# Group norm of a retention branch moved to GpSimd for both token tiles, with new orders in the third block

## The reference

```python
def chunkwise_retention(q, k, v):           # 8 heads of 64
    ...
    scores = jnp.einsum('bihd,bjhd->bhij', qc, kc) * inner_decay[None]
    ...

y = chunkwise_retention(qr, kr, vr)
mu = jnp.mean(y, axis=-1, keepdims=True)
var = jnp.mean(jnp.square(y - mu), axis=-1, keepdims=True)
y = ((y - mu) * lax.rsqrt(var + GN_EPS)).reshape(b, s, B_WIDTH)
y = y * ret_gn_w[l].astype(jnp.float32) + ret_gn_b[l].astype(jnp.float32)
out_b = (jax.nn.silu(gb.astype(jnp.float32)) * y).astype(x.dtype)
x = x + jnp.concatenate([out_a, out_b], axis=-1) @ w_out[l]
```

## Time and profile before

| what | before |
|---|---|
| device time, median of 3 runs (lowest, highest) | 911.14 us (911.08, 912.14) |
| the profiled execution | 912.54 us, of which the span from first to last instruction is 910.8 us |
| mean granted TensorE clock | 0.998 of full speed |
| PE busy | 900.0 us (99% of the span) |
| DVE busy | 608.3 us (67%) |
| ACT busy | 489.0 us (54%) |
| POOL busy | 65.5 us (7%) |
| HBM traffic | 177 GB/s over the span |

### The profile page before, as it was taken

One profiled execution on the slowest core, in us unless ns is written; L12 is line 12 of the kernel. 1 busy time (PEld: TensorE's weight loads), 2 busy tenths in 40 slices (PEclk: granted clock), 3 DMA queues, 4 the chain that ended last, 5 costly groups with the idle time before them and its releaser, 6 DMA issues.

```text
span 910.8 us, 13492 instructions
## 1 busy us (share of the span) xinstructions
PE 900.0 (99%) x4811; PEld 755.2 (83%) x4811; DVE 608.3 (67%) x927; ACT 489.0 (54%) x755; POOL 65.5 (7%) x124
## 2 busy tenths in 40 slices
PE   9999999999999999999999999999998999999998
PEld 8778788888888887768888888888886888888887
DVE  5868867555555687874755555668998666555565
ACT  7666756444444475873644444555577554444442
POOL 1311112000000010000200000012320000000000
PEclk9999999999999999999999999999999999999999
DMA  8935155655555551436755555436361446555541
GB/s 294 344 133 182 56 189 204 207 185 184 185 190 192 172 185 46 167 134 233 254 199 193 184 184 188 154 128 230 95 208 47 139 142 229 184 185 194 189 169 47
DMA packets 96884, 159.88 MB, mean 176 GB/s; under 512 B 5968, under 2 KB 37920, under 8 KB 96840
## 3 DMA queue, kind: packets, MB, share of 16 engines
q1 hardware_dynamic: 94240, 155.08, 51.1%
q10 hardware_dynamic: 2568, 4.21, 1.4%
q0 software_dynamic: 32, 0.02, 0.0%
HBM read 158.21 MB, written 3.16 MB: 177 GB/s over the span
## 4 chain that ended last, share of the span: by engine, by line
PE 94%; DVE 4%; ACT 1%; issue 1%; POOL 0%; DVEq 0%; POOLq 0%; ACTq 0%
PE turn L1754 10%; PE proj L1754 9%; PE proj L1698 6%; PE score L1698 6%; PE proj L1700 6%; PE proj L1699 6%; PE score L1699 6%; PE score L1700 6%; PE outp L1698 5%; PE outp L1700 5%; PE outp L1699 5%; PE turn L1758 5%; PE proj L1758 5%; PE turn L1744 2%; PE score L1896 1%; PE turn L1906 1%
## 5 line engine op out<-in xcount | busy, mean ns | idle before, releaser
L2027 DVE TENSOR_TENSOR wlo<-raw,whi 128x2048 fp32r<-128x2048 f32 (+1 forms) x131 | 297.2, 2278 | 167.5 <-ACT whi L1449 132.7
L1449 ACT ACTIVATE whi<-raw 128x2048 fp32r<-128x2048 f32 x64 | 122.7, 1917 | 162.6 <-PE turn L1758 76.2
L1438 ACT ACTIVATE whi<-raw 128x2048 fp32r<-128x2048 f32 (+1 forms) x67 | 126.2, 1895 | 60.7 <-PE score L1700 17.0
L1698 PE MATMUL proj<-whi,set 128*128 128x512 f32 (+2 forms) x266 | 104.9, 394 | 0.0
L1700 PE MATMUL proj<-whi,set 128*128 128x512 f32 (+2 forms) x266 | 102.2, 384 | 0.0
L1699 PE MATMUL proj<-wlo,set 128*128 128x512 f32 (+2 forms) x266 | 102.0, 383 | 0.0
L1754 PE MATMUL turn<-set,whi 128*128 128x512 f32 x384 | 96.3, 393 | 0.0
L1754 PE MATMUL proj<-set,whi 128*128 128x512 f32 x384 | 95.6, 391 | 0.0
L1698 PE MATMUL score<-whi,set 128*128 128x512 f32 x232 | 91.5, 394 | 0.0
L1699 PE MATMUL score<-wlo,set 128*128 128x512 f32 x232 | 90.6, 391 | 0.0
L1700 PE MATMUL score<-whi,set 128*128 128x512 f32 x232 | 90.4, 390 | 0.0
(11 more groups left out here) (252 smaller groups left out, 1283.9 us busy)
## 6 DMA issues: line engine op xcount, KB each, us to landing
raw<-in_a_w_up SPq DMA_DIRECT2D x32, 512.0 KB, 4.2
raw<-in_a_w_down SPq DMA_DIRECT2D x32, 512.0 KB, 4.5
raw<-in_b_w_up SPq DMA_DIRECT2D x32, 512.0 KB, 4.2
raw<-in_b_w_down SPq DMA_DIRECT2D x32, 512.0 KB, 4.6
raw<-in_w_gate SPq DMA_DIRECT2D x22, 512.0 KB, 4.0
raw<-in_w_up SPq DMA_DIRECT2D x22, 512.0 KB, 5.0
raw<-in_w_down SPq DMA_DIRECT2D x22, 512.0 KB, 3.9
raw<-in_a_w_in SPq DMA_DIRECT2D x20, 512.0 KB, 6.5
```

The lines of the kernel that those rows point to most:

```text
L1438: return act.activation(shaped(whi, u)[:, ks, :], shaped(raw, u)[:, ks, :], ACT.Copy)
L1449: act.activation(shaped(whi, u), shaped(raw, u), ACT.Copy).then_inc(hi_done, 1)
L1698: pe.matmul(out_, hi, wh, start=start, stop=False)
L2027: return dve.tensor_tensor(shaped(wlo, u)[:, ks, :], shaped(raw, u)[:, ks, :], shaped(whi, u)[:, ks, :], ALU.subtract)
```

## The change

The inverse root of the group norm (both tiles, 16 columns) goes from DVE to POOL, into the same function that the other statistics use, so a wait of POOL on DVE's sums and a wait of DVE on POOL's result are added. Weight, bias and gate of tile 1 go from DVE to POOL too, behind those of tile 0. And the orders of PE, DVE and ACT in the third block are different.

```diff
@@ in the list of steps @@
         group = add("group_square")
+        inverse_use(group)
         group.o, group.va, group.rs = last[1], col(16), col(16)
@@ POOL @@
                 elif st.kind == "shared_key_sum":
                     inverse_of_sums(st.st, st.st.rs, st.st.ss, DH)
+                elif st.kind == "group_sum":
+                    inverse_of_sums(st.st, st.st.rs, st.st.va, DH, GN_EPS)
                 elif st.kind == "group_gate":
-                    y = o_nat[:, 0, 512:1024]
-                    pool.wait_ge(yn_done, 1)
                     pool.wait_ge(gn_landed, 32)
-                    behind(pool.tensor_tensor(y, y, gn[:, 0, :], ALU.mult))
-                    behind(pool.tensor_tensor(y, y, gn[:, 1, :], ALU.add))
-                    pool.wait_ge(*st.st.gate)
-                    pool.tensor_tensor(y, y, zq[:, 1, 0, :], ALU.mult).then_inc(ob_done, 1)
+                    for t in range(NT):
+                        y = o_nat[:, t, 512:1024]
+                        pool.wait_ge(yn_done, t + 1)
+                        behind(pool.tensor_tensor(y, y, gn[:, 0, :], ALU.mult))
+                        behind(pool.tensor_tensor(y, y, gn[:, 1, :], ALU.add))
+                        pool.wait_ge(*st.st.gate)
+                        pool.tensor_tensor(y, y, zq[:, 1, t, :], ALU.mult).then_inc(ob_done, 1)
@@ DVE @@
                         ins = dve.tensor_reduce(group.va[:, 8 * t:8 * t + 8], heads_view(rt[:, t, :]), AX_X, ALU.add)
-                    behind(ins)
-                    inverse_rms(group.rs, group.va, DH, GN_EPS)
+                    ins.then_inc(sum_done, 1)
                 elif st.kind == "group_scale":
                     group = st.st
+                    wait_inverse(group)
                     for t in range(NT):
                         y = heads_view(o_nat[:, t, 512:1024])
                         dve.tensor_tensor(y, y, spread(group.rs[:, 8 * t:8 * t + 8], DH), ALU.mult).then_inc(yn_done, 1)
-                elif st.kind == "group_gain":
-                    y = o_nat[:, 1, 512:1024]
-                    dve.wait_ge(yn_done, 2)
-                    dve.wait_ge(gn_landed, 32)
-                    behind(dve.tensor_tensor(y, y, gn[:, 0, :], ALU.mult))
-                    behind(dve.tensor_tensor(y, y, gn[:, 1, :], ALU.add))
-                elif st.kind == "group_gate":
-                    y = o_nat[:, 1, 512:1024]
-                    dve.wait_ge(*st.st.gate)
-                    dve.tensor_tensor(y, y, zq[:, 1, 1, :], ALU.mult).then_inc(ob_done, 1)
@@ MOVES, two entries of many @@
-        ("turn_weights 32", "turn_weights 33"), ("multiply 70", "multiply 71"), ("turn_heads 27", "multiply 69"),
+        ("turn_weights 32", "turn_weights 33"), ("keep_busy 1", "turn_weights 32"), ("multiply 70", "multiply 71"),
```

## The result

The changed kernel takes 913.68 us (median of 19 executions, 912.91 to 914.84) against 912.14 us for the kernel before (19, 911.08 to 913.88): a ratio over all executions of 1.0019, 95% interval [1.0013, 1.0025]. By the medians it is 1.5 us slower where 1.3 us faster was forecast. The profiled execution took 914.48 us around a span of 912.7, against 912.54 around 910.8.

What follows compares the result with a forecast made beforehand. PE, busy 99% of the span, was taken as the bound, so only its waits or low clock could be won. 0.95 us at `multiply 72` plus 0.4 at weight transposes gave 1.3 off 911.14: 909.8 us, range 908.2 to 912.1.

Steps and rivals of the forecast that it cites:

- The DVE part: Ahead of `scores 16`: without Newton and the products, three search rounds from 674.8 and the scale leave DVE free 5.0 us earlier.
- POOL's inverse: Group norm's inverse root: power of 0.69 to 5.5 us at 16 columns, taken as within the 1.6 us covered, no cost.
- The third rival: Slower: POOL's power grows with its columns to 5.5 us, delaying scale, y and `multiply 72`; 913.2 us, chance 0.11.
- The cover: At the transposes of y: ACT comes for y at 689.3, at least 0.8 us after PE has it.
- Scores 16 come later: At `scores 16`: ACT's query copies stand behind the gate's first tile, a new wait of 0.55 us.
- From there to the output projection: `scores 16` to `multiply 72`: PE waits 1.3 us, not 2.07, then ACT's queue sets the pace; `multiply 72` 0.95 us earlier.
- The surplus of 0.4: At the eight weight transposes at 703.05: 1.46 us falls to 1.04 without ACT's weight copy there, 0.4 us won.
- Group norm on POOL: POOL's six products start where they did, at 679.58, and take 8.2 us, ending at 687.7 to 688.5; no cost.
- The other moves: Reordered steps ahead of the query transposes, bias loads and `statistics 6`: taken as zero, up to 0.5 us each if cover fails.
- the clock's price: After PE's idle, from 686 to 690: the low clock withheld at most 1.0 + 0.56 us of work.
- The total: Whole kernel: 1.3 us off the median of 911.14 gives 909.8 us.
- the median's smaller surroundings: Whole kernel: time outside the span taken as smaller in the 911.14 median than in the profiled execution, 912.54 around 910.8.

Runs made afterwards that it cites:

- e3: Changed kernel with GpSimd's power over 2 of the 16 columns, the other 14 inverse roots set to 1: 912.28 us, ratio to before 1.0006.
- e8: Changed kernel with 12 more identity transposes on TensorE in its wait for GpSimd's y: 913.34 us, ratio to before 1.0012.
- e1: Changed kernel's code with the whole table of orders of the kernel before: 913.77 us, ratio to before 1.0017.
- e11: Changed kernel with the orders of before up to the last projections ahead of `scores 16`, new orders behind: 912.36 us, ratio to before 1.0009.
- e9: Kernel before with 25 instead of 10 keep-busy transposes on TensorE ahead of `scores 17`: 911.23 us, ratio 1.0002.
- e5: Changed kernel with the inverse back on VectorE and the old orders, all six products still on GpSimd: 912.15 us, ratio to before 0.9997.
- e10: e5 with 6 and 7 more transposes on TensorE in its two waits ahead of the mixed weights' transposes: 912.20 us, ratio to before 1.0005.
- e12: e11 with ScalarE's copy of query head 29 as before, so only the late orders are new: 913.23 us, ratio to before 1.0018.
- e6: Changed kernel with GpSimd's power over 2 of the 16 columns and the old orders: 912.40 us, ratio to before 1.0003.
- e13: Kernel before, unedited, profiled once more: this execution took 913.10 us.
- e7: Changed kernel with GpSimd's power of 16 columns done twice: 917.30 us, ratio to before 1.0051.
- e14: e12 unedited, profiled once more: this execution took 912.15 us.

## Why the prediction was wrong

**The DVE part** held in its lengths, not in its start: the rounds take 0.98 each, from 675.88 and not 674.8 (0.37 is the start of the program, the rest the early moves). They end at 678.8, and the maxima begin as soon as the scores are there. That VectorE was free early was worth 1.12 us at `scores 17`.

**POOL's inverse** is the step that failed: "I take a power within that, no cost". It took 2.91 us where the rounds cover 1.6, and PE waited 1.59 us for y. With the power over 2 columns 0.80 us of `multiply 76` is won (e3 against e8, both at full clock), and 0.79 us of time. Between 2 and 16 columns a power costs (2.91 - 0.69)/14 = 0.16 us a column on top of some 0.37. I had bounds of 0.69 and 5.5 and took a value by likeness to other instructions (VectorE's small ones, a GpSimd product of 512 columns), none of which is a power. The only row on a power had 2 columns and could not tell a fixed cost from one by column.

**The third rival** had the right mechanism (the power, the scale behind it, y late, then a low clock), with the size of the power too high and, more to the point, the length from which it decides: not some 4 us, since 2.9 was enough. The cover had been counted as if nothing else were late.

**Scores 16 come later** (0.36 of wait, 0.5 forecast) and **From there to the output projection** up to ScalarE's chain (wait 1.26, forecast 1.3; table load ended at 684.06, weight copy 1.90) held in shape. Then the chain was no longer ScalarE's: y came late, its operand copy waited 1.18 us, and `multiply 72` came 1.28 later in place of 0.95 earlier. The surplus of 0.4 at the eight weight transposes went where it was (1.46 at 703.05 before, 1.09 at 705.15 now), but the eight at 699.93 take 1.46 now; with the clock kept (e8) both take 1.09.

**Group norm on POOL** failed at its start. "It starts where it did" assumed the loads where they were; they are issued when PE has turned the queries, which the early moves delayed by 0.46, and with a cheap power GpSimd started on them 0.57 later (e3). The power added 0.85. The length of the six products was right: 8.45, forecast 8.1 to 8.9. The cover of 0.8 us was smaller than the 1.42 of the late start, and the late turn then brought the low clock.

**The other moves**, taken as nothing, are the second step that failed. They cost 0.46 us at the turn of the queries (e1 and e11 against the changed kernel): inside the 0 to 0.5 named for each, at its bad end. The forecast looked for the cost at PE alone; through the loads and the sums it grew to 0.90 us of time at full clock (e11), as much as the power's. One part is visible, PE's wait of 0.33 at 630.41 for ScalarE to empty a bank.

**The clock.** The forecast kept the clock's price as it was. In the profiles it is 1.27 us of `multiply 76` in the changed kernel (e8), but 0.50 in the kernel before (e9) and 0.34 in e5 (e10): where VectorE's results are due soon after, waits for them swallow what the clock gives back. In the times of executions the step from 1.000 to 0.998 is 1.24 in the changed kernel and 0.49 in e5, which is near; in the kernel before it is 1.41, for which the profiles have no explanation.

**The total** started from a wrong reading: "the median's smaller surroundings". The surroundings are the same in every execution whose span is on record, 1.7 to 1.8 us on top of it. The execution of 912.54 us, whose waits and low clock the sum was made of, was itself some 1.4 us longer inside than the median of 911.14 from which 1.3 us was taken off. Full-clock executions of the kernel before have no low clock to win, and perhaps a shorter wait.

**The sum** at `multiply 76`, changed kernel against before, is +1.38 in the profiles. With both waits filled (e8 against e9) it is +0.61; the other 0.77 is the difference of 1.27 and 0.50. For the kernel before, both profiles are of its longer executions. At full clock the changed kernel is 1.83 us behind (913.03 against 911.20). The power is 0.79 of it (e3), the early moves with the copy of head 29 1.00 (e12). These two are not shown to add up: with neither (e5, and e6 with a narrow power) 0.5 us is left, which is the six products on GpSimd or something that only the short executions of the kernel before have.

Open is what makes those short. A candidate, not tested: in its three profiles (before, e13, and e9 with the filled wait) GpSimd's first product starts 0.03 to 0.07 us ahead of VectorE's product for the weight of tile 1, which then takes 1.77 to 1.81 us where the gate product took 0.68. If VectorE came first, the maxima would come about 1 us earlier. The changed kernel has no such product on VectorE. Open is also which of the early moves cost the 0.46.

## What to carry to other kernels

A price read at 2 columns says nothing about 16 until fixed and per-column cost are told apart; with ends a factor of eight apart, work out what the middle would do before calling the upper end a rival. A moved step carries its DMAs with it: ask what frees their buffer and when they land, not only when the engine is free. And a wait of PE costs twice if the clock falls behind it; filling it with transposes is cheap, but gives back only what no other engine's result takes. Last, put the profiled execution beside the others before adding up what its waits are worth: if it is longer than the median, part of what it shows is not in the median to be won.

## What the runs showed of the hardware

- GpSimd's power: 0.69 us for 128x2, 2.91 for 128x16 (2.90 in e7). Its other instructions of 16 columns take 0.20 to 0.22, one about every 0.3 us.
- GpSimd's products of 512 columns take 1.26 to 1.34 us in most rows and up to 1.60 beside VectorE's; VectorE's of 512 columns took 0.68. VectorE's of 256 columns, 0.43 alone, took up to 1.31 beside GpSimd's.
- The same kernel with the same wait of 1.4 us on TensorE ran at a granted clock of 1.00 in two profiles (e12, e14), and six of e12's eleven executions have a mean clock of 0.998; the kernel before lost its clock ahead of 686 in one profile (0.93 from 684 to 686, then 0.50) and a microsecond later in another (0.75 from 686 to 688, then 0.50). The Trainium skill's TensorE: Matmul & The Clock Gate, section "Part 1: The HAM clock gate (the "warmup" mystery)", says that the chip's watch on activity runs on freely and doesn't begin with the kernel, so that the same kernel can differ from run to run; these runs agree.
